# Branch merge: two weight groups worked together in pairs of PSUM banks

## Time and profile before

| | us |
|---|---|
| median of three runs | 2937.4 |
| the runs | 2934.73, 2937.4, 2942.89 |
| span of the profiled execution | 2936.0 |
| of it, the merge's 1152 products | 520.0 to 787.0 |
| granted TensorE clock, mean of the span | 0.976 |

### The profile page before, as it was taken

The page is one execution under the profiler, slowest core; times in us unless marked ns, Lnnn a source line. Parts: engine busy times, 40 slices in busy tenths (PEclk is TensorE's granted clock), DMA queues, the critical chain, the costliest instruction groups (busy, mean ns, idle before and its releaser), DMA issues.

```text
span 2936.0 us, 38234 instructions
## 1 busy us (share of the span) xinstructions
PE 2751.1 (94%) x13888; PEld 2054.4 (70%) x13902; DVE 1689.0 (58%) x3157; ACT 1404.4 (48%) x2557; POOL 210.9 (7%) x248
## 2 busy tenths in 40 slices
PE   7999999999993999999997998899999999999998
PEld 3467895788772777777765865676678775876776
DVE  1268463343457888888855559554643557546523
ACT  2343263232242666666646547644632458447422
POOL 0000000000000010000006000000020000000500
PEclk9989999999996999999998999999999999999999
DMA  9610020332425899999975300210041301000321
GB/s 372 211 58 29 29 87 1 115 114 87 160 108 193 300 373 375 375 377 378 377 249 146 84 15 8 59 44 30 16 144 61 112 1 59 29 19 20 116 86 58
DMA packets 178458, 401.60 MB, mean 137 GB/s; under 512 B 7948, under 2 KB 9004, under 8 KB 177792
## 3 DMA queue, kind: packets, MB, share of 16 engines
q1 hardware_dynamic: 158224, 329.27, 31.6%
q0 software_dynamic: 19936, 70.26, 7.4%
q10 hardware_dynamic: 144, 0.01, 0.0%
HBM read 363.70 MB, written 35.81 MB: 136 GB/s over the span
## 4 chain that ended last, share of the span: by engine, by line
PE 82%; DVE 9%; ACT 4%; issue 3%; DMA 2%; DVEq 0%; SPq 0%; POOLq 0%; POOL 0%; ACTq 0%
PE psum L303 8%; PE psum L790 7%; PE psum L792 7%; PE psum L791 7%; PE psum L1504 5%; PE psum L1502 5%; PE psum L1503 5%; PE psum L1642 4%; PE psum L1447 3%; PE psum L1446 3%; PE psum L1445 3%; PE psum L1660 3%; PE psum L1684 3%; PE psum L1745 2%; PE psum L1747 2%
## 5 line engine op out<-in xcount | busy, mean ns | idle before, releaser
L791 PE MATMUL psum<-ring_r,cols_r 128*128 128x512 f32 (+1 forms) x544 | 212.2, 390 | 0.0
L791 PE MATMUL psum<-ring_r,kctx_r 128*128 128x512 f32 (+1 forms) x544 | 211.8, 389 | 0.0
L2161 ACT ACTIVATE ring<-ring,att 128x256 f32<-128x256 f32 (+7 forms) x256 | 173.1, 676 | 33.8 <-DVE att L2812 33.8
L2666 DVE TENSOR_TENSOR ring_r<-ring,pair_r 128x1024 fp32r<-128x1024 f32 x128 | 148.1, 1220 | 47.4 <-ACT pair_r L2036 47.4
L1642 PE MATMUL psum<-wide 64*128 64x512 f32 (+2 forms) x704 | 147.9, 500 | 5.4 <-issue 2.5
L1503 PE MATMUL psum<-ring_r,wide_r 128*128 128x512 f32 x384 | 150.2, 391 | 0.0
L629 DVE TENSOR_TENSOR ring_r<-ring,ring_r 128x1024 fp32r<-128x1024 f32 x48 | 58.7, 1225 | 129.7 <-ACT ring_r L626 129.3
L1445 PE MATMUL psum<-small_r,ring_r 128*128 128x512 f32 x320 | 126.0, 394 | 0.8 <-DVE pair L2536 0.8
L1447 PE MATMUL psum<-small_r,ring_r 128*128 128x512 f32 x320 | 126.5, 395 | 0.0
L2036 ACT ACTIVATE pair_r<-ring 128x1024 fp32r<-128x1024 f32 x128 | 124.4, 1046 | 0.6 <-PE psum L1504 0.6
L1660 PE MATMUL psum<-ident,ring 128*128 128x128 f32 x640 | 116.7, 290 | 6.4 <-DVE ring L2839 6.3
(11 more groups left out here) (561 smaller groups left out, 7166.5 us busy)
## 6 DMA issues: line engine op xcount, KB each, us to landing
ring<-in_w_gate SPq DMA_DIRECT2D x64, 1024.0 KB, 9.7
ring<-in_w_up SPq DMA_DIRECT2D x32, 1024.0 KB, 9.9
hidden<-in_w_up SPq DMA_DIRECT2D x32, 1024.0 KB, 9.8
hidden<-in_w_down SPq DMA_DIRECT2D x32, 1024.0 KB, 8.6
pair<-in_w_down SPq DMA_DIRECT2D x32, 1024.0 KB, 8.9
ring<-in_w_ada SPq DMA_DIRECT2D x24, 1024.0 KB, 14.3
ring<-in_w_in SPq DMA_DIRECT2D x24, 1024.0 KB, 7.3
ring<-in_even_w_in SPq DMA_DIRECT2D x16, 1024.0 KB, 13.5
```

The source lines that it names most:

```text
L791: self.eng.matmul(outp, XHIGH[b][:, k, :], low[:, k, 0:wd], start=False, stop=False)
```

```diff
-            def merge_group(t, c, k0, kn, outp, high, low, ns):
+            def merge_pair(t, c0, k0, kn, outs, high, low, ns, done=None):
 
                 lows = ringr(slots[place[PASSES[t][2], PASSES[t][0], PASSES[t][1]]])
                 for k in range(k0, k0 + kn):
-                    if c == 0 and k % 2 == 0:
+                    if c0 == 0 and k % 2 == 0:
                         pe.wait_ge(S("mg_w_low"), before("mg_w_low") + 4 * t + k // 2 + 1)
-                    j, w = k - k0, HIGHS[:, k, span(c)]
-                    pe.matmul(outp, w, high[:, j, :], start=(j == 0), stop=False)
-                    pe.matmul(outp, w, low[:, j, ns], start=False, stop=False)
-                    mm = pe.matmul(outp, lows[:, k, span(c)], high[:, j, :], start=False, stop=(j == kn - 1))
-                    if c == 3 and k % 2 and k < KT - 1:
+                    j, last = k - k0, k == k0 + kn - 1
+                    for i in range(2):
+                        pe.matmul(outs[i], HIGHS[:, k, span(c0 + i)], high[:, j, :], start=(j == 0), stop=False)
+                    for i in range(2):
+                        pe.matmul(outs[i], HIGHS[:, k, span(c0 + i)], low[:, j, ns], start=False, stop=False)
+                    for i in range(2):
+                        mm = pe.matmul(outs[i], lows[:, k, span(c0 + i)], high[:, j, :], start=False, stop=last)
+                        if last and done:
+                            mm.then_inc(S(done), 1)
+                    if c0 == 2 and k % 2 and k < KT - 1:
                         mm.then_inc(S("mg_w_used"), 1)
-                return mm
 
             for t, (n, m, key) in enumerate(PASSES):
                 g, ns = 2 * n + m, slice(n * HALF, (n + 1) * HALF)
-                for c in range(4):
+                for c in (0, 2):
                     if key == "fm":
                         y = 4 * g + c
                         if c == 0 and m == 0:
                             pe.wait_ge(S("mg_x_low"), before("mg_x_low") + 8 * n + 8)
                         if y >= 2:
-                            pe.wait_ge(S("mg_mul"), 2 * (y - 1))
-                        b = 4 + 2 * (y % 2)
-                        merge_group(t, c, 0, 4, bank(b), FU_HIGH, FU_LOW, ns)
-                        merge_group(t, c, 4, 4, bank(b + 1), HM_HIGH, HM_LOW, ns).then_inc(S("mg_y"), 1)
+                            pe.wait_ge(S("mg_mul"), 2 * y)
+                        merge_pair(t, c, 0, 4, (bank(4), bank(6)), FU_HIGH, FU_LOW, ns)
+                        merge_pair(t, c, 4, 4, (bank(5), bank(7)), HM_HIGH, HM_LOW, ns, "mg_y")
                         continue
                     s = 8 * g + 4 * ("br1", "br2").index(key) + c
                     if s >= 4:
-                        pe.wait_ge(S("mg_sig"), s - 3)
+                        pe.wait_ge(S("mg_sig"), s - 2)
                     if c == 0 and m == 0 and key == "br1":
                         pe.wait_ge(S("mg_x_low"), before("mg_x_low") + 8 * n + 4)
-                    merge_group(t, c, 0, 8, bank(c), M_HIGH, M_LOW, ns).then_inc(S("mg_br"), 1)
+                    merge_pair(t, c, 0, 8, (bank(c), bank(c + 1)), M_HIGH, M_LOW, ns, "mg_br")
             pe.wait_ge(S("mg_sig"), 32)
```

## The result

| | before | after |
|---|---|---|
| median, us | 2934.73 (5 runs, 2929.29 to 2942.89) | 3002.35 (5 runs, 3002.10 to 3007.36) |
| ratio, 95% interval | | 1.0229 (1.0217 to 1.0241) |
| span of the profiled execution | 2936.0 | 3000.5 |
| mean granted clock of the span | 0.976 | 0.970 |

The account below looks back on a forecast made before the run. TensorE (PE), busy 94% of the span, was taken as the bound. Waits 52.8 + clock 23.8 + pitch 0 = 76.6 us, added to 2936.0, gave 3012.6; the runs' median lies 1.4 higher, so 3014.0, range 2986 to 3028.

Parts of the forecast that it names:

- The pitch: Start-to-start time of merge products: claimed unchanged at 0.232 us, effect 0, bounds -6.9 to +9 us.
- End of a branch pass: Ends of br1 and br2 passes: next weights' roundings queue behind c = 2's sigmoid; 2.99 us lost, 8 times, 23.9.
- E: Start of a pass's last product; its partner's last product starts 0.23 us earlier.
- Middle of an fm pass: Second pair waits for multiplications of c = 0 and 1 to free banks; 3.42 us lost, 4 times, 13.7.
- E': Start of the first pair's last product in an fm pass.
- End of an fm pass: DVE's subtractions for the next pass stand behind merged(2); 3.36 us lost, 3 times, 10.1.
- Tail: After the last pass: first output job at E + 4.62, second at E + 12.4 instead of 7.3; 5.1 us lost.
- Sum of waits: All PE waits in the merge and after its last pass: 23.9 + 13.7 + 10.1 + 5.1 = 52.8 us.
- The clock: Half-speed stretches of 3.4 us after merge stalls: 14 x 1.7 = 23.8 us lost; stage clock about 0.93.
- I take 14: Of 15 merge stalls, 14 were counted as followed by a lowered clock costing 1.7 us each.
- The bounds: Limits for clock lowering, 0 and 25.5 us; pitch, -6.9 and +9; likeliest case 3000 to 3027; longer pitch to 3036.
- The rival with a clock that holds: Merge stalls leave the clock unlowered, so only the waits count: 2937.4 + 52.8 = 2990 us; chance 0.17.

## Why the prediction was right, point by point

The forecast was 3014.0 us with a range of 2986 to 3028; measured were 3002.35. The forecast stood 79.3 us above the median of the five runs of before, of which 76.6 were the change; 67.6 came.

- *The pitch, 0.* Right: 0.232 us with one bank, with two, and with or without shared rows.
- *End of a branch pass, 8 times.* Forecast: PE's next start at E + 3.11. Measured from the starts in the changed kernel's trace, E + 3.21 or 3.22 for each of the eight. The first step after it is 0.31, not 0.34.
- *Middle of an fm pass, 4 times.* Forecast E' + 3.54, measured 3.53.
- *End of an fm pass, 3 times.* Forecast E + 3.48, measured 3.56 or 3.57.
- *Tail.* Forecast 4.62 and 12.4 after E, measured 850.53 - 845.83 = 4.70 and 858.22 - 845.83 = 12.39 (the last pair starts at 845.60, its second product 0.23 later).

```profile
845.60 0.63 PE L1450 MATMUL psum<-small_r,ring_r 128*128 128x512 f32 x2
850.53 0.77 PE L790 MATMUL psum<-ring_r,kctx_r 128*128 128x512 f32 x1 [4.30 <-DVE ring_r L773]
...
858.22 0.50 PE L790 MATMUL psum<-ring_r,cols_r 128*128 128x512 f32 x1 [0.33 <-DVE wide_r L759]
```

- *Sum of waits.* Forecast 52.8. Measured 8 x (3.21 - 0.23) + 4 x (3.53 - 0.23) + 3 x (3.56 - 0.23) = 47.0, with 15 x 0.08 = 1.2 for first steps 48.2, and 12.39 - 7.3 = 5.1 for the tail: 53.3. The run that keeps the clock up measured 53.1.
- *The clock.* This term was too large: forecast 14 lowerings at 1.7 us, 23.8. The trace shows nine after the fifteen stalls (the merge grew by 62.5 us from first to last start, less 48.2 of waits leaves 14.3, 1.6 each), and a tenth in the tail, which costs nothing there, as forecast. The step that failed is "I take 14": I read from two gaps, 2.88 with and 2.06 without a mark, that 2.7 would nearly always leave one. By the same term the stage was to last 339 us at a clock of 0.93, and it lasted 329.6 at 0.95.
- *The bounds.* By the terms given, 15 lowerings and the longest pitch make 2937.4 + 52.8 + 25.5 + 9 = 3025, not 3027, and no sum gives the 3036. Nothing here rests on either.

The miss of 9 us in the change's cost is this one term, 23.8 - 14.3 = 9.5, less 0.5 by which the waits were longer than forecast. The rival with a clock that holds would have given 2990, 12 us below; the truth lay about midway between it and the forecast. That the waits came out to 0.5 us is the mechanism; that the total is inside the range owes something to a range wide enough for both cases. The Trainium skill's warning about idle gaps (TensorE: Matmul & The Clock Gate, "Why this matters for your kernels") would let gaps of 2.8 us pass: the trace disagrees, since the stall of 2.82 us that ended at 541.98 was followed by half clock from 543.2 on. The 216 ns which the same page gives for 512 columns ("Back-to-back issue gap") were reached by no group of fp32r products in any order tried: the least here was 0.227 on average. For the bf16 products that filled the waits the trace agrees: their starts are 0.215 or 0.216 us apart.

## What to carry to other kernels

When products are regrouped so that results arrive later and in pairs, look first in the queues of the other engines for what stands *behind* the evacuation of those results: here it was the next pass's operands, and the wait landed on TensorE though in the changed stage neither engine was busy a third of the time (ACT 75.94 and DVE 91.48 of 329.60 us). Work for the next pass belongs ahead of work on the last group, and a pair of outputs needs its banks twice, once to fill and once to drain. A full engine (here 266.98 of 267.00 us) can only lose by a reordering that leaves its work and its pitch as they are; measure the pitch, from start to start, before trading buffers for it.

## What the runs showed of the hardware that I had not expected

Stalls of the same length are not all followed by the lower clock. In the changed kernel a gap of 2.82 us (to 541.98) was, and one of 2.81 us (to 568.88) and one of 3.17 us (to 599.43) were not; the windows behind 543 and 569 above show 0.52 and 1.00. Nine of fifteen stalls left a mark there, nine of eleven in the kernel with other banks, ten of eleven in the one with the late announcement, whose stalls are 0.23 longer. What else than the length decides was not isolated; that the same gaps fall differently in time in each kernel is the only difference seen, and an argument, not a test. Filling the gaps with bf16 products brought the clock of the merge to 1.00 and saved the 14 us, without shortening a wait.

The pitch of fp32r products of 512 columns changed clearly only with the rows that were streamed or with where they lay: 5.44, 5.57 or 5.62 us for 24 of them. Neither the PSUM bank nor shared rows moved its average by more than 1 ns. The bf16 products of the filled waits, also 512 columns wide, start 0.216 us apart, but they differ in type, weights and rows at once, so which of these makes them faster is open.
